# A hybrid DeltaNet / RWKV-7 / PEER step on one core: fourteen gate tiles under the substitution, and the off-diagonal blocks of 36 triangular inverses joined in one step

## The reference

```
P = rmsnorm(x, ln1) @ w_in                     # q,k,v,z | beta,alpha | r,kr,vr,w,a,g | gate a, gate b
# DeltaNet branch, 4 heads, in chunks:
A   = strict_lower(kb @ k.T * decay) + I       # one triangular matrix per head and chunk
sol = triangular_solve(A, rhs)                 # unit diagonal
# sample tokens: S = S * exp(g); kv = S.T k; delta = (v - kv) * beta; S += outer(k, delta); o = S.T q
# RWKV-7 branch, 8 heads: S = S * w + (S a) b' + v k'; y = S r
m   = sigmoid(ga) * (o_dn @ w_up_dn) + sigmoid(gb) * (o_rw @ w_up_rw)
h   = x + m @ w_out
# PEER: top 16 of 128 x 128 product keys for 8 heads per token, then
h   = h + sum_k gate_k * gelu(u[e_k] . xn) * v[e_k]       # rows of u and v (4 KB each) gathered
y   = rmsnorm(h, ln_f)
```

## Time and profile before

| | us |
|---|---|
| median of 3 runs | 1171.31 (1167.8 to 1172.44) |
| the profiled execution | 1169.43 |
| its span, first to last instruction | 1167.7 |
| mean granted TensorE clock | 0.974 of full |
| PE busy | 996.7 (85%) |
| DVE busy | 713.6 (61%) |
| POOL busy | 518.8 (44%) |
| ACT busy | 270.0 (23%) |

### The profile page before, as it was taken

How to read it: one execution, slowest core, us unless ns; L and a number is a source line. 1 busy time by engine, 2 the same in 40 slices (tenths; PEclk the granted TensorE clock), 3 DMA queues, 4 the chain that set the end, 5 groups by cost and what they waited for, 6 DMA issues and landing times.

```text
span 1167.7 us, 11377 instructions
## 1 busy us (share of the span) xinstructions
PE 996.7 (85%) x3771; PEld 566.7 (49%) x3771; DVE 713.6 (61%) x1879; ACT 270.0 (23%) x643; POOL 518.8 (44%) x580
## 2 busy tenths in 40 slices
PE   6999998989999998997997777777777777777788
PEld 5886677879997554763442222222222222222221
DVE  1025763985363626994756766765776776676553
ACT  2146544015233012211112111111121111111111
POOL 2000100000000004667577677777767777777763
PEclk9999989989997998998999999999999999999999
DMA  8342022450353617999999999999999999999997
GB/s 283 108 150 73 1 75 54 129 175 2 73 190 115 205 47 270 405 365 368 410 409 401 408 408 409 404 410 406 409 397 400 410 408 410 408 408 408 392 371 277
DMA packets 120824, 334.26 MB, mean 286 GB/s; under 512 B 19103, under 2 KB 35330, under 8 KB 120502
## 3 DMA queue, kind: packets, MB, share of 16 engines
q0 software_dynamic: 76032, 276.86, 60.2%
q1 hardware_dynamic: 44602, 56.64, 15.0%
q10 hardware_dynamic: 132, 0.04, 0.0%
HBM read 326.99 MB, written 5.74 MB: 285 GB/s over the span
## 4 chain that ended last, share of the span: by engine, by line
PE 34%; DMA 27%; DVE 20%; POOL 11%; issue 5%; ACT 2%; SPq 0%; DVEq 0%; POOLq 0%; ACTq 0%
PE bank L1408 32%; DMA sb_all<-in_peer_u,idx 17%; POOL sb_all L586 11%; DMA sb_all<-in_peer_v,idx 9%; DVE sb_all L1126 5%; ACT sb_all L1812 2%; DVE sb_all L1104 1%; DVE sb_all L1102 1%; DVE sb_all L1106 1%; DVE sb_all L2297 1%; DVE sb_all L2294 1%; DMA sb_all<-in_w_in 1%; DVE key_i L1074 1%; DVE sb_all L1067 1%; DVE key_i L1068 1%
## 5 line engine op out<-in xcount | busy, mean ns | idle before, releaser
L1408 PE MATMUL bank<-sb_all 128*128 128x512 f32 (+15 forms) x3462 | 964.2, 430 | 148.0 <-DMA sb_all<-in_peer_v,idx 132.7
L1408 PEld LDWEIGHTS bank<-sb_all 128*128 128x128 f32 (+7 forms) x3462 | 537.5, 186 | 569.3 <-DMA sb_all<-in_peer_v,idx 315.9
L1126 DVE CUSTOM_DVE_ANT_0 sb_all<-sb_all,bank 128x1024 f32<-128x1024 f32 x264 | 314.5, 1220 | 185.3 <-DMA sb_all<-in_peer_u,idx 185.0
L586 POOL DMA_INDIRECT sb_all<-in_peer_u,idx x264 | 252.0, 955 | 217.8 <-DVE idx L1110 103.2
L586 POOL DMA_INDIRECT sb_all<-in_peer_v,idx x264 | 253.9, 962 | 88.6 <-issue 66.4
L1812 ACT ACTIVATE sb_all<-sb_all 128x128 f32<-128x128 f32 (+10 forms) x367 | 144.9, 420 | 557.6 <-PE bank L1408 368.1
L1812 ACT ACTIVATE sb_all<-bank 128x264 f32<-128x264 f32 (+16 forms) x183 | 82.8, 468 | 323.7 <-PE bank L1408 273.3
L621 POOL IOTA sb_all<- 128x54 f32 x1 | 0.2, 184 | 162.8 <-PE bank L1408 162.8
L1398 POOL MEMSET sb_all<- 128x3456 f32 x1 | 3.0, 2986 | 131.5 <-DVE sb_all L2208 131.5
L2091 DVE SCALAR_TENSOR_TENSOR sb_all<-sb_all 128x288 f32<-128x288 f32 x14 | 6.1, 516 | 63.1 <-ACT sb_all L1812 63.1
L1812 ACT ACT_TABLE_LOAD x22 | 28.2, 1283 | 7.5 <-DVE sb_all L2229 3.9
(11 more groups left out here) (231 smaller groups left out, 423.6 us busy)
## 6 DMA issues: line engine op xcount, KB each, us to landing
sb_all<-in_w_in SPq DMA_DIRECT2D x8, 2048.0 KB, 7.8
sb_all<-in_peer_wq SPq DMA_DIRECT2D x4, 2048.0 KB, 17.6
sb_all<-in_w_in SPq DMA_DIRECT2D x5, 1024.0 KB, 5.1
sb_all<-in_peer_u,idx POOLq DMA_INDIRECT x264, 10.8
sb_all<-in_peer_v,idx POOLq DMA_INDIRECT x264, 10.8
out<-sb_all SPq DMA_DIRECT2D x8, 512.0 KB, 4.0
sb_all<-in_w_out SPq DMA_DIRECT2D x2, 2048.0 KB, 8.1
sb_all<-in_x_prompt SPq DMA_DIRECT2D x4, 512.0 KB, 4.0
```

The lines of the kernel that those rows point to most:

```text
L586: pool.indirect_dma_start(ring[at % 8], None, table[0], bass.IndirectOffsetOnAxis(ap=idx[:, c:c + 1], axis=0)).then_inc(landed[at % 8], 16)
L1126: v.tensor_tensor_reduce(uring[i % 8], uring[i % 8], x, 1.0, 0.0, ALU.mult, ALU.add, hdot[:, u % 2, j:j + 1]).then_inc(u_free, 1)
L1408: return nc.tensor.matmul(out, lhsT, rhs, start=start, stop=stop, **kw)
```

## The change

Two changes are merged, and several smaller moves come with them.

- **One step in place of two levels.** One unit per four matrices, 9 in all, computes X - XNX + XNXNX with N all blocks below the diagonal (one mask). `inv_right` is replaced by `inv_once` (only columns 32 to 95) and `inv_twice` (32 x 32 out of 64 rows); ACT copies a third piece (`zz`, 64 x 128) and negates `yy`; DVE adds two results (96 x 256 and 32 x 128) instead of one subtraction.
- **Fourteen fill tiles.** Gate tile 13 is computed with the others under the substitution; its weights come in a separate piece. It is left in PSUM and copied out by ACT after the joining. `gate_tile(1, 0)` in chunk 0 is gone.
- **beta and alpha** are computed in four pieces, one after each tile of kr; the 14 transposes stand between q's second and third tile.
- **The root of kk's norm** is taken after the first k tile instead of the second, and the taps on DVE are regrouped around its reciprocal.
- **Sample states.** The products with k and q use k and q as the stationary operand (16 columns, all but two of them zero, built by POOL in `sdm`) and the state as the moving one (128 columns), summed over the 8 samples in PSUM; ACT copies 16 x 512 (`mvt`), PE turns them back in four transposes after the first up-projection tile. `pst` stands behind the last transposes instead of ahead of the sample products.

```diff
-        UNITS_INV = [(l, g, q) for l in (LEVELS - 1, LEVELS) for g in range(3) for q in range(3)]
+        UNITS_INV = [(g, q) for g in range(3) for q in range(3)]
-        IN_PARTS = {"g1": 256, "g2": 256, "g3": 128}
+        IN_PARTS = {"g1": (256,), "g2": (256,), "g3": (128, 128)}
-        FILL = [(name, f) for name in ("g0", "g1", "g2") for f in range(4)] + [("g3", 0)]
+        FILL = [(name, f) for name in ("g0", "g1", "g2") for f in range(4)] + [("g3", 0), ("g3", 1)]
...
# PE, projections
+                    if name == "kr":
+                        small_projection(f)
-            for c in range(NCH + 1):
-                cols, n = (ccols(c), TC) if c < NCH else (slice(NP, NC), NS)
-                for k in range(KT):
-                    ins = mm(psv(4, n, 8, at=8 * c), xnT[:, k, cols], wba[:, k, :], start=k == 0, stop=k == KT - 1)
-            ins.then_inc(ba_ready.sem, 1)
+            project("q", part=(0, 2))
             pe.wait_ge(ba_used.sem, ba_used.at(1))
...
-            project("q")
+            project("q", part=(2, 4))
...
# PE, joining the blocks
-            def inv_right(u):
+            def inv_once(u):
                 pe.wait_ge(inv_y_used, u + 1)
-                if u >= 2:
-                    pe.wait_ge(inv_z_used, u - 1)
+                if u == 2:
+                    pe.wait_ge(proj_used, 43)
+                if u >= 3:
+                    pe.wait_ge(inv_z_used, u - 2)
                 for n in range(4):
-                    ins = mm(psv(4 + u % 2, TC, TC, at=TC * n), yy[0:TC, 4 * (u % 3) + n, :], xT[0:TC, 12 * g + 4 * q + n, :])
+                    ins = mm(psv(4 + u % 3, TC, 64, at=TC * n + 32), yy[0:TC, 4 * (u % 3) + n, :],
+                             xT[0:TC, 12 * g + 4 * q + n, 32:TC])
                 ins.then_inc(inv_z, 1)
+            def inv_twice(u):
+                pe.wait_ge(inv_part.sem, inv_part.at(u + 1))
+                for n in range(4):
+                    m = 4 * (u % 3) + n
+                    ins = mm(psv(4 + u % 3, 32, 32, at=4 * TC + 32 * n), yy[0:64, m, 0:32], zz[0:64, m, :])
+                ins.then_inc(inv_sum.sem, 1)
-            for u in range(NU + 2):
+            for u in range(NU + 3):
                 if u < NU:
                     inv_turn(u)
                 if 1 <= u < NU + 1:
                     inv_left(u - 1)
-                if u >= 2:
-                    inv_right(u - 2)
+                if 2 <= u < NU + 2:
+                    inv_once(u - 2)
+                if u >= 3:
+                    inv_twice(u - 3)
...
# PE, recurrence and sample branch
                     right_side(0).then_inc(rw_r, 1)
-                    gate_tile(1, 0)
...
+            pe.wait_ge(consts, 3)
+            pe.wait_ge(dn_s_done, NCH)
             for h in range(DH):
                 for b in range(NS):
-                    ins = mm(psv(3, 128, 2, at=2 * (8 * h + b)), st[:, 8 * h + b, :], sd[:, h:h + 5:4, b])
+                    ins = mm(psv(3, 16, 128, at=128 * h), sdm[:, h, 16 * b:16 * b + 16], st[:, 8 * h + b, :],
+                             start=b == 0, stop=b == NS - 1)
...
# ACT, joining the blocks
+                if u >= 2:
+                    act.wait_ge(inv_z, u - 1)
+                    w = 4 * ((u - 2) % 3)
+                    fn(zz[0:64, w:w + 4, :], psv(4 + (u - 2) % 3, 64, 4, TC)[:, :, 64:TC]).then_inc(inv_part.sem, 1)
...
# DVE, joining the blocks
-                dve.wait_ge(inv_z, u + 1)
-                tt(x4, x4, psv(4 + u % 2, TC, 4, TC), ALU.subtract).then_inc(inv_z_used, 1)
                 if u + 3 < NU:
                     inv_coupling(u + 3)
+                dve.wait_ge(inv_sum.sem, inv_sum.at(u + 1))
+                step(tt(x4[:, :, 32:TC], x4[:, :, 32:TC], psv(4 + u % 3, TC, 4, TC)[:, :, 32:TC], ALU.add))
+                step.sync()
+                tt(x4[0:32, :, 64:TC], x4[0:32, :, 64:TC], psv(4 + u % 3, 32, 4, 32, at=4 * TC), ALU.add).then_inc(inv_z_used, 1)
...
# DVE and ACT, around the norm of kk
-            taps(0, range(4), tap_q)
+            taps(0, (0, 1), ((tap_q, 1), (tap_q, 2)))
             dve.wait_ge(kk_root.sem, kk_root.at(1))
             v.reciprocal(kk_norm[0:8], kk_norm[0:8]).then_inc(kk_inv.sem, 1)
-            taps(1, (4, 5), tap_ka)
+            taps(0, (2, 3), ((tap_q, 3), (tap_q, 4)))
+            taps(1, (4, 5), ((tap_ka, 1), (tap_kb, 1)))
```

More of the change, by code:

```diff
@@ L1358, in _ @@
             odd = []
[L1359 to L1365 removed]
+            for b in (32, 64):
+                n = min(b, TC - b)
+                odd.append((level[:, LEVELS, b:b + n].rearrange("p (m r) -> p m r", m=1), b, 1))
             for v, b, m in odd:
@@ L1437, in project, with small_projection @@
                     tile[0] += 1
+                    if name == "kr":
+                        small_projection(f)
+            def small_projection(c):
+                cols, n = (ccols(c), TC) if c < NCH else (slice(NP, NC), NS)
+                for k in range(KT):
+                    ins = mm(psv(4, n, 8, at=8 * c), xnT[:, k, cols], wba[:, k, :], start=k == 0, stop=k == KT - 1)
+                if c == NCH:
+                    ins.then_inc(ba_ready.sem, 1)
             pe.wait_ge(xT_done, 8)
@@ L1804, in _ @@
             turn_rw(NCH - 1, 4)
+            pe.wait_ge(rw_s_done, NCH)
+            for f in range(4):
+                for s in range(2):
+                    ins = mm(psv(7, 64, 128, at=128 * f), s_rw_p[:, f, 64 * s:64 * s + 64], ident, start=s == 0, stop=s == 1)
+            ins.then_inc(pst_t, 1)
             pe_rest(pe, mm, project)
@@ L1958, in _ @@
             evacuate(zs[3:4], ACT.Silu, NX, banks=4)
-            for n in range(len(FILL)):
+            for n in range(len(FILL) - 1):
                 act.wait_ge(proj_ready, tile[0] + 1)
@@ L1962, in _ @@
                 tile[0] += 1
-            for u in range(NU + 1):
+            for u in range(NU + 2):
                 if u < NU:
```

139 lines of the change are left out of this document (72 added, 67 removed).

## The result

The changed kernel takes 1150.37 us (median of 4, 1147.51 to 1152.8) against 1170.75 of before on the same chip: ratio 0.9823, 95% interval 0.9804 to 0.9841. A second session gave 0.9805 (0.9789 to 0.9821). It is faster, by some 20 us instead of the 33.9 of the sum. The profiled execution took 1150.32, its span 1148.6.

A forecast was written before the change was run, and what follows sets the result against it. The path to POOL's first gather, mostly PE and its clock, bounds the kernel. Gains 1.4 + 5.0 + 15.5 + 3.6 + 8.4 = 33.9 off 1169.4 give 1135.5, as a median 1137 us; range 1129 to 1150.

The forecast's parts named there:

- Part 1a: Projections, beta and alpha matmuls moved: ACT ready earlier for q's last tile, gain 1.4 us (bounds 0 and 2.2).
- Part 1b: Projections, earlier root of kk: PE's 3.06 us wait goes, plus 1.95 of clock; gain 5.0 (bounds 3.1 and 5.4).
- Part 2: Joining of the blocks in one step: nine rounds of 2.0 us at full clock, gain 15.5 (bounds 8.7 and 16).
- Part 3: Recurrence: gate tile 13 leaves chunk 0 and PE goes on without a wait; gain 3.6 (bounds 2.5 and 3.6).
- Part 4: Sample branch: state products in 7.2 us at full clock, `pst` off the path; gain 8.4 (bounds 3.5 and 9).
- Rival A: The low clock moves to other places instead of going: 1145 us, at worst 1152; chance 0.17.
- Rival C: Small products let the clock fall in the joining and the recurrence never wins it back: 1202 us; chance 0.03.
- Cost 0: Fill ahead of the joining: the 14th tile fits into PE's 3.09 us wait for the DMA, costing nothing.
- Rival B: Hand-overs between engines, not PE, bind the joining: rounds of 3 us, 1146 us; chance 0.12.
- Rival D: The fill's 14th tile is late because its weights are; joining starts up to 3 us later, 1140 us; chance 0.06.

The follow-up runs named there:

- e4: Changed kernel without the 32x32 products and the second add (term XNXNX left out, so values differ): 1146.5 us, ratio 0.9803.
- e3: Changed kernel plus two unused wide products on PE in the 1.12 us gap ahead of the recurrence: 1142.0 us, ratio 0.9766.
- f2: Changed kernel plus two unused wide products in the gap ahead of the recurrence and 16 memsets on POOL: 1139.7 us, ratio 0.9738.
- g1: Changed kernel plus two wide filler products in the low-rank gap, two ahead of the recurrence, and 16 memsets on POOL: 1140.1 us, ratio 0.9734.
- g3: Changed kernel with gate tile 13 back in chunk 0 and seven unused wide products in its place at the fill's end: 1149.6 us, ratio 0.9834.
- h5: Kernel before plus five memsets on POOL, one execution: first gather 3.39 us behind the indices.
- h2: Kernel before with only the new one-step joining of the block rows, 13 fill tiles: 1174.6 us, ratio 1.0042.
- e2: Changed kernel with gate tile 13 back in chunk 0 and 13 fill tiles: 1165.2 us, ratio 0.9965.

## Why the prediction was wrong, step by step

- **What bounds the kernel, and that everything behind the first gather stays**: right.
- **Part 1a, forecast 1.4, got -2.4: wrong.** The sum moved q earlier but asked only when ACT would be ready for q's last tile. The next row in line was the low-rank products: PE reached them at 90.1, ran four and stood 0.97 us for ACT's first copy, and ran at 0.50 for 6.8 us behind that (3.4). "Their 32 small matmuls only move, so PE's own work stays" was no cover.
- **Part 1b, forecast 5.0**: the wait of 3.06 went, right; the 1.95 of clock did not come in the changed kernel (118.4 to 121.7 at 0.50 as before), though undoing 1b shows more clock lost. Its lower bound, "the clock falls all the same", was what the trace shows.
- **Part 2, forecast 15.5, got 14.0: right in mechanism, one term mis-sized.** It came to 15.5 - 1.5: the small products at 0.30 a round measure 0.50, and rounds 2.17 instead of 2.0. I had sided with the 0.0375 of 8-column instructions, and for the spacing that was about right: the small ones start 0.036 apart on average. What the term left out is the change from one shape to the next, some 0.26 us a round (e4). The rule in the Trainium skill, TensorE: Matmul & The Clock Gate, section "Back-to-back issue gap" (about 62 ns per matmul with hardware decode off), would have given the right sum, 0.50 a round, but the trace does not agree with it: these matmuls start 32 ns apart, about half of 62, so the case for which the rule is stated is not this one.
- **Part 3, forecast 3.6, got -1.3: the step that failed most.** "So without the tile PE goes on with no wait" was true of the waits. But the 1.12 us that PE stands ahead of the recurrence, which I had in the sum as time and not as a gap, was followed by 10.2 us at 0.50 where there had been none (before, PE stood 0.73 there): 5.1 lost on 3.6 won. e3, f2 and g1 show that filling the gap brings it back; g3 shows that the tile in chunk 0 would not have, though its stretch is shorter (6.8).
- **Part 4, forecast 8.4, got 6.3.** The products themselves were sized right, 7.22 at full clock in f2 against 7.2; in the changed kernel they took 8.71 with 3.4 us at 0.50, where the forecast had said "The clock should stay"; behind the filled gap it did in e3 and f2, and not in g1. The remaining 0.6 lies in the short steps around them and was not tried.
- **The first gather, -2.2, was in no part of the sum.** "Done some 10 us before PE asks" covered POOL's new instructions by their duration. That they shift the code behind them was not thought of, and the count of instructions is all that made the difference in h5.
- **Rival A (0.17) is what happened.** By the table 16.5 are missing from the 33.9 (the profiled executions show 14.8, the early start having given 1.85). Of these 11.9 are clock (1a 3.4, 1b 1.9, chunk 0 5.1, state products 1.5), 1.5 the small products with the changes around them, 2.2 the gather, and 0.9 short steps. A was priced at 8, at worst 15 (1152): it counted the clock that would not come back, and too little for new low stretches.
- **Rival C (0.03) did not come, but was close.** In h2 and e2 the clock does stay low through the joining, though not as C had it: it falls behind the idle time of 3.3 to 3.4 us at the joining's start, and the rounds with small products then run at 0.50 to their end. In the changed kernel they run at 1.00. What kept the clock up was one tile that the forecast counted as "Cost 0". **Rival B** is refuted: no hand-over holds PE in the rounds. **Rival D** too: PE goes through the fill (239.75 to 252.44) and into the transposes with no idle time.
- **The range** ended at 1150, 0.4 us below the time. The lower bounds gave 1153.5, and I cut them as "all at once and unlikely"; they were not independent, since the clock stands in three of the five. And two parts came out below their own bounds, 1a (-2.4 against 0) and 3 (-1.3 against 2.5), because neither bound had a new low stretch in it. (Part 2's bound, 8.7, is 8.9 by its own terms, and part 4's "7.0 earlier" is 6.9; neither matters here.)

## What to carry to other kernels

Where PE waits a microsecond and narrow products follow, look at the clock behind the wait before pricing the wait: a filler of two wide products in a gap of 1.1 us gave 5 to 6.5, and a filler of 3 us decided whether a restructured stage of 20 us was worth 14 or less than nothing. Moving work away from in front of such a stage is a change of the stage. And an edit on an engine that sleeps until a critical moment shifts its code: look at the distance from the releaser to the released instruction in both traces, and if it grew with "issue" as the reason and a packet of the kind "instruction" lies between, add or drop an instruction or two and look again.

## What the hardware showed that was not expected

- A stage of 96x64 and 32x32 products, entered after 3.4 us without work, stayed at 0.50 for 41.0 us with PE busy 31 to 32 of 32 us (e2, h2); the same stage entered behind wide products ran at 1.00 throughout. With 96x96 products alone the clock was back after 6.8 us, 3.4 to 10.2 in further executions. The Trainium skill, TensorE: Matmul & The Clock Gate, section "What's actually happening", has the low clock as the default that activity releases. These runs do not bear that out if activity is what PE's row shows as busy: 31 to 32 of 32 us were, and the clock stayed down until 264-column products came.
- Eight matmul instructions of 64x32 by 32 columns between 96-row ones lengthen a round by 0.50 us at full clock: they start 32 ns apart, and about half of the 0.50 lies at the two changes of shape.
- Where a packet of the kind "instruction", 8 KB, lies between the releaser and POOL's next instruction, that instruction is 2.2 us late or more (ten of ten traces; none of the nine others). It comes and goes with a single instruction more or less (five added: late; four or six: not).
